# Latent attention weighed with the keys on the partitions, and retention's splits in another order: a two-block transformer forward on one core

## The chip, the cores and the metric

The kernel is one program on one core of a Trainium2 chip. The metric is the device time of one execution in microseconds (us), and the time of a kernel is the median of its runs. The engines are named as in the profile: PE (TensorE, matmuls), PEld (its weight loads), DVE (VectorE), ACT (ScalarE), POOL (GpSimd) and SP (SyncE, which issues most DMAs).

## The reference, cut to what matters

A first block of two layers is followed by a second block of two layers (short convolution, sparse attention, experts). The change touches the two mixers of the first block, on T = 16 + 512 = 528 tokens in float32:

```python
# layer 0: latent attention, 8 heads, 64 + 32 query/key dims, 64 value dims
q = (_rmsnorm(p_q, q_norm_g) @ w_uq); kv = (_rmsnorm(p_kv, kv_norm_g) @ w_ukv)
q = concat([q_nope, _rope(q_pe)]);  k = concat([k_nope, _rope(k_pe), one for all heads])
s = einsum('bqhd,bkhd->bhqk', q, k) * 96 ** -0.5;  s = where(kpos <= qpos, s, -1e30)
o = einsum('bhqk,bkhd->bqhd', softmax(s), v)
mix = concat([y_rec, o]) @ ev_w_out
# layer 1: retention, 4 heads of 256 query/key and 512 value dims
q, k = _rope(q), _rope(k) / 16
o = (q k^T * decay) v                      # kernel: over all 528 tokens at once
o = o * rsqrt(mean(o * o) + EPS);  mix = (silu(g) * o) @ od_w_out
```

## The kernel before, in words

Each engine has its own program, written as one function for each stage and engine (`mla_pe`, `mla_act`, `mla_dve`, `mla_pool` for latent attention, `ret_*` for retention, `out0_*` for the projection behind attention). An engine works in the order of its function, and semaphores join the engines. A `Signal.mark` says what an instruction has done and `wait_ge` waits for it. PSUM places are given out by a `Ring`: `take` waits until the last holder of the place is read out (`emptied`). `PS` are four places of two banks, `BANK` the eight single banks.

**Large products** (`dense`) run on weights split into a high and a low half. ACT casts a 128-column part of the loaded weights to its high half (`split_hi`), DVE subtracts it to get the low half (`split_lo`), and PE waits for the low half of each part. There are three places for parts (`WS`), and the splits run two parts ahead of PE: a call of `split_hi` and `split_lo` in an ACT or DVE function makes the next part in the list. Activations are split in the same way; `x_hi` and `x_lo` say when a row group is ready. The first two output tiles of a `dense` are done as a pair, row group k by row group k.

**Latent attention.** Features lie on the partitions. For each head PE projects q (96 rows) and k (64 rows), ACT copies them out, and PE turns q for the rotary part; DVE and POOL multiply, and DVE adds. All 8 heads are projected first, then v for five token blocks `TT` (four of 128 and one of 16). Then 40 query blocks x (head x // 5, block x % 5) go through a pipeline: scores for x + 3 (queries on the partitions), the mask, the row maximum and its scaling on DVE, the exponential with its sum on ACT into `P0` for x + 2, transposes of the probabilities on PE and the copy to `PT` on ACT for x + 1, and probabilities times v for x, one 64-column product per key block. DVE takes the reciprocal of the sum and scales the output into `OT`; every second head `turn_out_*` transposes 128 output features into place for `out0`.

**Retention**, for each head h: two q tiles, two k tiles, two plus two v tiles (`vg_cols`, first half), four g tiles, each 128 features wide; then transposes of v, scores, decay and the weighted sum. While head h starts, the output of head h - 1 is squared, normalised and multiplied into `YR` (POOL, `ret_scaled_pool`). Each engine then waits for these products (`pool_rot["y", h - 1, f]`), because `vT` is written again. DVE rotates q and k, and only then comes the loop over the v and g tiles with its splits. Behind head 3 the mean square goes through PE (`ret_norm_pe`), 16 row groups of `YR` are split into `HS` (k < 8) and `YS`, and the projection `("out", 1)` starts.

## Time and profile before

| | |
|---|---|
| median of 3 runs | 3312.5 us (3302.4 to 3315.7) |
| profiled execution, its own time | 3316.9 us |
| its span, first to last instruction | 3315.1 us |
| mean granted PE clock, of full speed | 0.936 |
| latent attention, first projection to the projection behind it | 132.98 to 294.77 us |
| of which projections of q, k and v | 132.98 to about 170 us |
| retention with its output projection's start | 749.61 to 1161.14 us |

Times in rows are microseconds from the span's start. Busy PE is not PE at its peak, because the ends of matmuls are modelled; the distance between starts says more. A float32 product counts as two matmul instructions. The granted clock is a share of 2.4 GHz, so 0.50 is 1.2 GHz. The number in square brackets or behind the second bar is the time an engine sat idle before the instruction, with what ended it.

### The profile page before, as it was taken

Reading aid. Unit: us, or ns where it says so; the run is one execution under the profiler, and the core shown is the slowest. Engines: PE = TensorE matmul, PEld = TensorE weight load, DVE = VectorE, ACT = ScalarE, POOL = GpSimd, SP = SyncE. Lnnn points to the kernel's source line nnn. Section 1 sums busy time; section 2 is a strip of 40 time slices with the busy share of each in tenths; the row PEclk is TensorE's granted clock in tenths of the full one; section 3 lists DMA queues with packets and bytes.
Section 4 is the critical chain, followed back from the end, with each engine's and each line's share of the span. In section 5 each row is a group of like instructions: output and inputs, shape, how many; then the busy total and the mean of one; then the engine's idle time right before and its main releaser. Section 6 shows DMA issues by size and latency. Waiting matters only on the chain.

```text
span 3315.1 us, 42753 instructions
## 1 busy us (share of the span) xinstructions
PE 2974.9 (90%) x17700; PEld 2318.1 (70%) x17700; DVE 1432.2 (43%) x2550; ACT 906.6 (27%) x1620; POOL 598.2 (18%) x529
## 2 busy tenths in 40 slices
PE   7899999999999899999999798888698897988884
PEld 6667999998887687888787455555476684555552
DVE  4543432334444434333444453333488845533334
ACT  3432422323222324232323121111334621211111
POOL 1201300112111012011200342222000002522220
PEclk9967899999999999999999899999899998999997
DMA  4010222222221132322222999999621019999996
GB/s 134 17 61 26 77 90 90 90 90 86 68 65 57 51 96 82 101 90 97 81 89 70 375 408 409 410 408 408 242 89 58 21 38 357 406 408 410 409 409 270
DMA packets 271813, 600.30 MB, mean 181 GB/s; under 512 B 32375, under 2 KB 177202, under 8 KB 255226
## 3 DMA queue, kind: packets, MB, share of 16 engines
q1 hardware_dynamic: 247408, 569.47, 45.6%
q0 software_dynamic: 23968, 27.93, 2.6%
q8 instruction: 144, 2.36, 0.3%
q14 instruction: 59, 0.48, 0.0%
q10 hardware_dynamic: 234, 0.06, 0.0%
HBM read 607.75 MB, written 39.89 MB: 195 GB/s over the span
## 4 chain that ended last, share of the span: by engine, by line
PE 85%; DVE 6%; issue 4%; DMA 2%; ACT 1%; POOL 1%; SPq 0%; DVEq 0%; POOLq 0%; ACTq 0%
PE ps L101 78%; PE ps L104 6%; POOL sb_arena L118 1%; DVE sb_arena L126 1%; DVE sb_tmpA L118 1%; DMA sb_ring<-in_exp_w_dram 1%; DVE sb_tmpA L126 1%; DVE sb_tmpA L122 1%; DVE sb_arena L118 0%; SPq L144 0%; DMA sb_arena<-x_rows,sb_smallu 0%; DVE sb_tmpA L2000 0%; ACT sb_hs L112 0%; DMA sb_arena<-in_ln_b_dram 0%; DVE sb_ws L118 0%
## 5 line engine op out<-in xcount | busy, mean ns | idle before, releaser
L101 PE MATMUL ps<-sb_hs,sb_ws 128*128 128x264 f32 (+1 forms) x6384 | 1117.3, 337 | 31.1 <-DVE sb_ws L118 17.6
L101 PEld LDWEIGHTS ps<-sb_hs,sb_ws 128*128 128x128 f32 x6384 | 982.7, 192 | 162.5 <-DVE sb_ws L118 18.5
L118 DVE TENSOR_TENSOR sb_ws<-sb_ring,sb_ws 128x1024 fp32r<-128x1024 f32 x279 | 367.6, 1321 | 433.9 <-ACT sb_ws L112 433.5
L101 PE MATMUL ps<-sb_arena 128*64 128x256 f32 (+16 forms) x2068 | 394.1, 438 | 48.5 <-issue 29.7
L112 ACT CAST sb_ws<-sb_ring 128x1024 fp32r<-128x1024 f32 x279 | 290.6, 1046 | 373.4 <-PE ps L101 355.4
L101 PE MATMUL ps<-sb_ring,sb_arena 128*64 128x256 f32 (+2 forms) x2314 | 324.0, 436 | 56.4 <-issue 55.2
L101 PE MATMUL ps<-sb_br,sb_ws 128*128 128x264 f32 (+1 forms) x2304 | 366.5, 321 | 0.0
L101 PEld LDWEIGHTS ps<-sb_br,sb_ws 128*128 128x128 f32 x2304 | 332.3, 188 | 33.7
L101 PEld LDWEIGHTS ps<-sb_arena 128*64 128x64 f32 (+6 forms) x2068 | 232.9, 170 | 154.0 <-issue 87.0
L101 PEld LDWEIGHTS ps<-sb_ring,sb_arena 128*64 128x64 f32 (+1 forms) x2314 | 196.7, 148 | 150.7 <-issue 88.8
L104 PEld LDWEIGHTS ps<-sb_cst,sb_arena 128*128 128x128 f32 (+3 forms) x1032 | 156.6, 206 | 195.7 <-DVE sb_arena L118 82.3
L101 PE MATMUL ps<-sb_hx,sb_arena 128*64 128x256 f32 (+1 forms) x1536 | 245.1, 470 | 27.4 <-issue 27.3
L108 ACT ACTIVATE sb_arena<-ps 64x256 f32<-64x256 f32 (+2 forms) x148 | 60.2, 407 | 765.0 <-PE ps L101 761.1
L118 DVE TENSOR_TENSOR sb_arena<-sb_arena,ps 64x256 f32<-64x256 f32 x128 | 54.3, 424 | 488.2 <-ACT sb_arena L108 488.2
L104 PE MATMUL ps<-sb_cst,sb_arena 128*128 128x128 f32 (+3 forms) x1032 | 203.2, 325 | 63.5 <-DVE sb_arena L123 22.1
L2448 POOL DMA_INDIRECT y_rows<-sb_arena,sb_smallu x128 | 134.6, 1052 | 660.9 <-PE ps L104 477.3
L112 ACT COPY sb_arena<-ps 128x128 f32<-128x128 f32 (+6 forms) x377 | 150.2, 435 | 328.3 <-PE ps L101 276.7
L101 PEld LDWEIGHTS ps<-sb_hx,sb_arena 128*64 128x64 f32 x1536 | 127.0, 144 | 102.8 <-issue 65.9
L118 POOL TENSOR_TENSOR sb_tmpA<-sb_tmpA 128x528 f32<-128x528 f32 (+1 forms) x88 | 103.2, 1173 | 461.6 <-ACT sb_tmpA L108 461.6
L115 DVE COPY sb_arena<-ps 64x512 f32<-64x512 f32 (+4 forms) x160 | 110.8, 695 | 152.9 <-PE ps L101 131.2
L2444 POOL DMA_INDIRECT sb_arena<-x_rows,sb_smallu x128 | 133.5, 1043 | 78.1 <-issue 35.6
L101 PE MATMUL ps<-sb_ys,sb_ws 128*128 128x512 f32 x576 | 139.3, 399 | 7.0 <-DVE sb_ws L118 7.0
(186 smaller groups left out, 2177.0 us busy)
## 6 DMA issues: line engine op xcount, KB each, us to landing
sb_ring<-in_exp_w_dram SPq DMA_DIRECT2D x160, 1024.0 KB
sb_hx<-in_exp_w_dram SPq DMA_DIRECT2D x128, 1024.0 KB
sb_arena<-in_exp_w_dram SPq DMA_DIRECT2D x96, 1024.0 KB
sb_ring<-in_mlp_w_dram SPq DMA_DIRECT2D x64, 1024.0 KB
sb_ring<-in_od_w_in_dram SPq DMA_DIRECT2D x24, 1024.0 KB
sb_ring<-in_conv_w_in_dram SPq DMA_DIRECT2D x12, 1024.0 KB
sb_ring<-in_attn_w_in_dram SPq DMA_DIRECT2D x10, 1024.0 KB
sb_ring<-in_od_w_out_dram SPq DMA_DIRECT2D x8, 1024.0 KB
```

The source lines that it names most:

```text
L101: return self.e.matmul(o, l, r, start=start, stop=stop, skip_group_check=True)
L104: return self.e.transpose(o, i, ident)
L108: return self.e.activation(o, i, fn, bias=bias, scale=scale)
L112: return self.e.copy(o, i)
L115: return self.e.tensor_copy(o, i)
L118: return self.e.tensor_tensor(o, a, b, op)
L122: return self.e.tensor_scalar(o, a, s1, None, op0)
L126: return self.e.scalar_tensor_tensor(out=o, in0=a, scalar=s, in1=b, op0=op0, op1=op1)
L2444: return e.e.indirect_dma_start(dst, None, Xh, bass.IndirectOffsetOnAxis(ap=ig[:, b:b + 1], axis=0), bounds_check=1023, oob_is_err=False)
L2448: return e.e.indirect_dma_start(Yh, bass.IndirectOffsetOnAxis(ap=isc[:, b:b + 1], axis=0), src, None, bounds_check=2047, oob_is_err=False)
```

## The change

Latent attention keeps the pass over query blocks, now 16 queries first and then four of 128 (`TQ`), but only for the maximum and the sum: the exponentials are thrown away. The logarithm of the sum is taken for four heads at a time (`ln`), joined with the maximum (`lse`), transposed to rows (`l`) and sent by DMA to partition 96 of q (`QH`); partition 96 of k (`KT`) holds ones. A second pass (`t`) computes the scores again with the keys on the partitions and 97 rows contracted, so that their exponential is the finished probability; three groups of key blocks a head. Step `o` multiplies v by them, with up to 264 queries moving, and `e` reads out two heads at once. Transposes of probabilities and outputs, their copies, the reciprocals and the scaling are gone. All engines follow one order, `mla_order`, in which the first pass of heads 0 to 3 lies between the projections.

In retention, the split of the third part behind the k tiles moves ahead of the wait for `pool_rot["y", ...]`. Behind head 3, row groups 0 to 7 are split before the outputs are copied, 8 to 11 before the normalisation, 12 to 15 after it, and `ret_norm_pe` runs inside the first pair of `("out", 1)`, at its row group 4. `ret_dve` gets the same edits as `ret_act`, with `split_lo` and `late_lo`. Below, the code is indented by 8 columns less, and the removed lines of latent attention are left out.

```diff
 def dense(e, stage, cols, K, rhs, T, units, pair=True, between=None):
...
         for k in range(kn + 2):
+            if k == 4 and between is not None:
+                between()
...
+PT = ar.take(2, 1360)
+triT = ar.take(128)
+LROW = tmpA[0:4, 2:4, :]
+rots = (tmpA[0:96, 5, :], tmpA[0:96, 4, :])
...
+TQ = [(0, 16)] + [(16 + 128 * i, 128) for i in range(4)]
+den, mxs, nms, lse = (sm[:, 100 + 40 * i:140 + 40 * i].rearrange("p (i h) -> p i h", i=5) for i in range(4))
+P_AT = (0, 528, 928, 1200, 1344)
...
+    t0, tn = TQ[i]
...
+def col(tile, x):
+    h, i, t0, tn, n = qblock(x)
+    return tile[0:tn, i, h:h + 1]
+def mla_order():
+    yield from (("q", 0), ("q", 1), ("turn", 0), ("q", 2), ("turn", 1))
+    for h in range(4):
+        for i in range(3):
+            yield "s", 5 * h + i
+        yield "q", h + 3
+        yield "s", 5 * h + 3
+        yield "turn", h + 2
+        yield "s", 5 * h + 4
+    yield from (("ln", 0), ("q", 7), ("turn", 6), ("v", 0), ("lse", 0), ("v", 1), ("turn", 7), ("l", 0))
+    yield from (("v", 2), ("v", 3), ("v", 4))
+    for x in range(20, 25):
+        yield "s", x
+    x = 25
+    for k in range(26):
+        if k < 24:
+            yield "t", k
+        if k == 7:
+            yield "lse", 1
+        for _ in range(3 - k % 2 if k < 6 else 0):
+            yield "s", x
+            x += 1
+        if k == 5:
+            yield "ln", 1
+        if k >= 2:
+            yield "o", k - 2
+        if k == 8:
+            yield "l", 1
+        if k >= 2 and k % 6 == 1:
+            yield "e", k // 6 - 1
...
+    proj = Ring([PS[0], PS[1]], U_, emptied)
+    rows = Ring([PS[2], PS[3]], U_, emptied)
+    cols = Ring([BANK[0], BANK[1]], U_, emptied)
+    outs = Ring([PS[1]], U_, emptied)
+    u = proj.take(e, "triT")
+    e.tp(u[:, 0:128], tri, ident).then_inc(*turned.mark("triT"))
...
+    for step, x in mla_order():
+        if step == "q":
+            u = proj.take(e, ("qh", x))
...
+            u = proj.take(e, ("kh", x))
...
+        if step == "turn":
+            u = proj.take(e, ("qturn", x))
+            e.wait_ge(*act_emptied["qh", x])
...
+                t = e.mm(o, rmat[0:96, 0:96], QH[0:96, x, a:b], True, True)
+            t.then_inc(*turned.mark(("qturn", x)))
+        if step == "v":
+            t0, tn = TT[x]
+            u = proj.take(e, ("vt", x))
...
+            if x == 4:
+                proj.drain(e)
+        if step == "s":
+            h, i, t0, tn, n = qblock(x)
+            u = rows.take(e, ("s", x))
...
+            t.then_inc(*scored.mark(("mla", x)))
+        if step == "l":
+            u = rows.take(e, ("lse", x))
+            e.wait_ge(*dve_soft["lse", x])
+            for i, (t0, tn) in enumerate(TQ):
+                at = t0 if i < 4 else 512
+                t = e.tp(u[0:4, at:at + tn], lse[0:tn, i, 4 * x:4 * x + 4], ident[0:tn, 0:tn])
+            t.then_inc(*turned.mark(("lse", x)))
+        if step == "t":
+            h, c = x // 3, x % 3
+            if x == 12:
+                rows.drain(e)
+                held = cols.holder
+                cols = Ring([BANK[0], BANK[1], BANK[6], BANK[7]], U_, emptied)
+                cols.holder[0:2] = held
+                outs = Ring([PS[2], PS[1]], U_, emptied)
+                outs.holder[1] = ("o", 1)
+            u = cols.take(e, ("t", x))
+            e.wait_ge(*pool_rot["one"])
+            e.wait_ge(*lse_in[h // 4][h])
+            K, Q1 = KT[0:97, h, :], QH[0:97, h, :]
+            if c == 0:
+                t = e.mm(u[:, 0:512], K[:, 0:128], Q1[:, 0:512], True, True)
+            if c == 1:
+                e.mm(u[:, 0:400], K[:, 128:256], Q1[:, 128:T1], True, True)
+                e.mm(u[:, 400:416], K[:, 0:128], Q1[:, 512:T1], True, True)
+                t = e.mm(u[0:16, 416:432], K[:, 512:T1], Q1[:, 512:T1], True, True)
+            if c == 2:
+                e.mm(u[:, 0:272], K[:, 256:384], Q1[:, 256:T1], True, True)
+                t = e.mm(u[:, 272:416], K[:, 384:512], Q1[:, 384:T1], True, True)
+            t.then_inc(*scored.mark(("t", x)))
+        if step == "o":
+            h, c = x // 3, x % 3
+            if h % 2 == 0 and c == 0:
+                u_o = outs.take(e, ("o", h // 2))
+            p0 = 64 * (h % 2)
+            (oa, _, _), (ob, _, _) = split(u_o, T1, p0, p0 + 64)
+            p = PT[:, h % 2, :]
+            e.wait_ge(*act_emptied["t", x if c else x + 1])
...
+                    e.wait_ge(*act_emptied["vt", j])
+            for j in ((0,), (1, 4), (2, 3))[c]:
+                q0, jn = 128 * j, TT[j][1]
+                v, pj = Vt[0:jn, j, 64 * h:64 * h + 64], p[0:jn, P_AT[j]:P_AT[j] + T1 - q0]
+                if q0 < 264:
+                    e.mm(oa[:, q0:264], v, pj[:, 0:264 - q0], j == 0, j == 2)
+                a = max(q0, 264)
+                t = e.mm(ob[:, a - 264:264], v, pj[:, a - q0:T1 - q0], j == 0, j == 3)
...
+    cols.drain(e)
+    units.n = 2
+    units.holder[1] = ("o", 3)
...
+    for step, x in mla_order():
+        if step == "q":
+            if x == 0:
+                e.wait_ge(*turned["triT"])
+                e.acp(triT, U_["triT"][:, 0:128]).then_inc(*act_emptied.mark("triT"))
+            e.wait_ge(*summed["qh", x])
+            e.acp(halves(QH[0:96, x, :]), whole(U_["qh", x], T1, 0, 96)).then_inc(*act_emptied.mark(("qh", x)))
+            e.wait_ge(*summed["kh", x])
+            e.acp(halves(KT[0:64, x, :]), whole(U_["kh", x], T1, 0, 64)).then_inc(*act_emptied.mark(("kh", x)))
+        if step == "v":
+            tn = TT[x][1]
+            e.wait_ge(*summed["vt", x])
+            e.acp(Vt[0:tn, x, :], U_["vt", x][0:tn, 0:512]).then_inc(*act_emptied.mark(("vt", x)))
+        if step == "s":
+            h, i, t0, tn, n = qblock(x)
+            e.wait_ge(*dve_soft["max", x])
+            if x >= 2:
+                e.wait_ge(*act_emptied["s", x - 2])
+            e.act(tmpA[0:tn, x % 2, 0:n], U_["s", x][0:tn, 0:n], ACT.Exp, scale=SC96, bias=col(nms, x),
+                  acc=col(den, x)).then_inc(*act_emptied.mark(("s", x)))
+        if step == "ln":
+            e.wait_ge(*act_emptied["s", 20 * x + 19])
+            d = den[:, :, 4 * x:4 * x + 4]
+            e.act(d, d, ACT.Ln).then_inc(*act_soft.mark(("ln", x)))
+        if step == "l":
+            u = U_["lse", x]
+            e.wait_ge(*turned["lse", x])
+            e.acp(LROW[:, x, 0:400], u[0:4, 0:400]).then_inc(*act_emptied.mark())
+            e.acp(LROW[:, x, 400:T1], u[0:4, 512:640]).then_inc(*act_emptied.mark(("lse", x)))
+            e.wait_ge(*act_emptied["lse", x])
+            for i in range(4):
+                h = 4 * x + i
+                e.dma(QH[96:97, h, :], LROW[i:i + 1, x, :]).then_inc(
+                    *lse_in[x].land(*(range(4 * x, 4 * x + 4) if i == 3 else [])))
+        if step == "t":
+            h, c = x // 3, x % 3
+            u, p = U_["t", x], PT[:, h % 2, :]
+            e.wait_ge(*dve_soft["mask", x])
+            if h >= 2:
+                e.wait_ge(*weighed["mla", 3 * h - 4])
+            if c == 0:
+                e.act(p[:, 0:512], u[:, 0:512], ACT.Exp, scale=SC96).then_inc(*act_emptied.mark(("t", x)))
+            if c == 1:
+                e.act(p[:, 528:928], u[:, 0:400], ACT.Exp, scale=SC96).then_inc(*act_emptied.mark())
+                e.act(p[:, 512:528], u[:, 400:416], ACT.Exp, scale=SC96).then_inc(*act_emptied.mark())
+                e.act(p[0:16, 1344:1360], u[0:16, 416:432], ACT.Exp, scale=SC96).then_inc(
+                    *act_emptied.mark(("t", x)))
+            if c == 2:
+                e.act(p[:, 928:1344], u[:, 0:416], ACT.Exp, scale=SC96).then_inc(*act_emptied.mark(("t", x)))
+        if step == "e":
+            e.wait_ge(*weighed["mla", 6 * x + 5])
+            e.acp(halves(HS[:, 0, 4 + x, :]), whole(U_["o", x], T1)).then_inc(*x_hi.mark(("mix0", 4 + x)))
...
+    e.mset(sm[:, 100:260], 1.0).then_inc(*dve_soft.mark())
+    e.wait_ge(*dve_soft.now)
+    for step, x in mla_order():
+        if step == "q":
+            if x == 0:
+                e.wait_ge(*dve_lru["kpe"])
+            e.cp(KT[64:96, x, :], kpe[64:96, :]).then_inc(*dve_soft.mark(("kpe", x)))
+        if step == "turn":
+            rot = rots[x % 2]
+            e.wait_ge(*turned["qturn", x])
+            if x > 1:
+                e.wait_ge(*dve_soft["q", x - 2])
+            e.tt(halves(rot), whole(U_["qturn", x], T1, 0, 96), halves(S96[0:96, :]), ALU.mult).then_inc(
+                *dve_emptied.mark(("qturn", x)))
+            e.wait_ge(*dve_emptied["qturn", x])
+            e.wait_ge(*pool_rot["q", x])
+            e.tt(QH[0:96, x, :], QH[0:96, x, :], rot, ALU.add).then_inc(*dve_soft.mark(("q", x)))
+        if step == "s":
+            h, i, t0, tn, n = qblock(x)
+            u = U_["s", x]
+            e.wait_ge(*scored["mla", x])
...
+            e.rmax(col(mxs, x), u[0:tn, 0:n]).then_inc(*dve_soft.mark())
...
+            e.ts(col(nms, x), col(mxs, x), -SC96, None, ALU.mult).then_inc(*dve_soft.mark(("max", x)))
+        if step == "lse":
+            g = slice(4 * x, 4 * x + 4)
+            e.wait_ge(*act_soft["ln", x])
+            e.stt(lse[:, :, g], den[:, :, g], -1.0 / SC96, mxs[:, :, g], ALU.mult, ALU.subtract).then_inc(
+                *dve_soft.mark(("lse", x)))
+        if step == "t":
+            u = U_["t", x]
+            e.wait_ge(*scored["t", x])
+            e.wait_ge(*act_emptied["triT"])
+            e.tt(u[:, 0:128], u[:, 0:128], triT, ALU.add).then_inc(
+                *dve_soft.mark(*([("mask", x)] if x % 3 == 0 else [])))
+            if x % 3 == 1:
+                e.tt(u[0:16, 416:432], u[0:16, 416:432], triT[0:16, 0:16], ALU.add).then_inc(
+                    *dve_soft.mark(("mask", x)))
+            if x % 3 == 2:
+                e.tt(u[:, 272:400], u[:, 272:400], triT, ALU.add).then_inc(*dve_soft.mark(("mask", x)))
+        if step == "e":
+            hi, lo = HS[:, 0, 4 + x, :], HS[:, 1, 4 + x, :]
+            e.wait_ge(*x_hi["mix0", 4 + x])
+            e.tt(halves(lo), whole(U_["o", x], T1), halves(hi).bitcast(F), ALU.subtract).then_inc(
+                *dve_emptied.mark(("o", x)))
...
+    e.wait_ge(*dve_lru["h", 3])
+    e.mset(KT[96:97, :, :], 1.0).then_inc(*pool_rot.mark("one"))
+    for step, x in mla_order():
+        if step == "turn":
+            e.wait_ge(*turned["qturn", x])
+            e.tt(QH[0:96, x, :], QH[0:96, x, :], C96[0:96, :], ALU.mult).then_inc(*pool_rot.mark(("q", x)))
...
+        x_lo["mix0", k] if k < 4 else dve_emptied["o", k - 4])
...
-    ret_norm_pe(e, units, 3)
-    dense_all(e, ("out", 1), C4, 16, mix1_x, T2, units)
+    dense_all(e, ("out", 1), C4, 16, mix1_x, T2, units, True, lambda: ret_norm_pe(e, units, 3))
...
 def ret_act(e):
+    def late_hi(ks):
+        for k in ks:
+            e.wait_ge(*pool_rot["y", k // 4, k % 4])
+            e.acp(late(mix1_of(k, 0)), late(YR[:, k, :])).then_inc(*x_hi.mark(("mix1", k)))
+
...
+        split_hi(e)
         if h > 0:
             for f in range(4):
                 e.wait_ge(*pool_rot["y", h - 1, f])
-        for m in tiles(vg_cols(h)):
-            split_hi(e)
+        for n, m in enumerate(tiles(vg_cols(h))):
+            if n > 0:
+                split_hi(e)
...
+        if h == 3:
+            late_hi(range(8))
         for f in range(4):
             e.wait_ge(*weighed["ret", h, f])
...
     ret_squares_act(e, 3)
-    for k in range(8):
-        e.wait_ge(*weighed["ret", 3, 3])
-        e.wait_ge(*pool_rot["y", k // 4, k % 4])
-        e.acp(late(HS[:, 0, k, :]), late(YR[:, k, :])).then_inc(*x_hi.mark(("mix1", k)))
+    late_hi(range(8, 12))
     ret_scaled_act(e, 3)
...
+    late_hi(range(12, 16))
     for m in range(8):
         out_splits(e, split_hi, m)
         square_act(e, ("out", 1), m, 2)
```

## Rows read from the trace of the kernel before

**Rows 1.** The page: the span, and the engines' shares of the chain that ended last.

```profile
span 3315.1 us, 42753 instructions
...
PE 85%; DVE 6%; issue 4%; DMA 2%; ACT 1%; POOL 1%; SPq 0%; DVEq 0%; POOLq 0%; ACTq 0%
```

**Rows 2.** TensorE in order of time, stretches of latent attention: start, length, [idle before].

```profile
138.38 2.98 PE L101 MATMUL ps<-sb_arena,sb_ring 128*96 128x264 f32 x12
141.29 1.13 PE L101 MATMUL ps<-sb_arena,sb_cst 96*96 96x264 f32 x4
...
173.90 1.12 PE L101 MATMUL ps<-sb_arena 96*128 96x512 f32 x2
174.86 0.38 PE L104 MATMUL ps<-sb_cst,sb_arena 128*128 128x128 f32 x2
...
294.77 35.47 PE L101 MATMUL ps<-sb_hs,sb_ws 128*128 128x264 f32 x276 [1.43 <-DVE sb_hs L118]
```

**Rows 3.** Windows: length, busy us (instructions) by engine, PE clock, DMA share, GB/s.

```profile
133.00:170.00 37.00, 35.62 (x138) 20.23 (x138) 20.04 (x32) 12.72 (x21) 11.76 (x9) 1.00 0.09 29
170.00:184.00 14.00, 11.64 (x71) 7.55 (x70) 9.11 (x36) 6.18 (x21) 0.00 (x0) 1.00 0.95 301
206.00:240.00 34.00, 31.99 (x121) 21.69 (x121) 13.35 (x54) 10.47 (x33) 0.00 (x0) 0.50 0.00 1
294.80:298.00 3.20, 3.20 (x14) 3.20 (x15) 1.23 (x1) 0.12 (x1) 0.00 (x0) 0.50 0.00 0
298.00:301.00 3.00, 3.00 (x26) 3.00 (x26) 0.00 (x0) 0.00 (x0) 0.00 (x0) 0.99 0.00 0
882.40:892.00 9.60, 9.60 (x56) 9.60 (x57) 3.51 (x4) 0.68 (x1) 0.00 (x0) 0.68 0.34 111
2540.00:2580.00 40.00, 33.08 (x211) 24.45 (x211) 34.23 (x133) 25.67 (x72) 2.68 (x5) 1.00 0.16 41
```

**Rows 4.** Groups of VectorE instructions from 133 to 295 us, by shape.

```profile
L118 DVE TENSOR_TENSOR ps<-ps,sb_cst 128x128 f32<-128x128 f32 x32 | 9.3, 289 | 16.1 <-PE ps L101 16.1
L138 DVE TENSOR_REDUCE sb_small<-ps 16x1 f32<-16x528 f32 x8 | 5.6, 695 | 0.3
L122 DVE TENSOR_SCALAR sb_small<-sb_small 128x1 f32<-128x1 f32 x32 | 4.9, 153 | 1.1
L118 DVE TENSOR_TENSOR sb_arena<-ps,sb_arena 96x528 f32<-96x528 f32 x4 | 2.8, 704 | 5.0 <-PE ps L101 5.0
```

**Rows 5.** Groups of ScalarE instructions from 133 to 295 us, by shape.

```profile
L109 ACT ACTIVATION_READ_ACCUMULATOR sb_arena<-ps,sb_small 128x1 f32 x32 | 6.2, 194 | 0.0
L109 ACT ACTIVATE sb_arena<-ps,sb_small 128x512 f32<-128x512 f32 x8 | 5.5, 687 | 2.2 <-DVE sb_small L122 2.2
```

**Rows 6.** Groups of GpSimd instructions from 133 to 295 us, by shape.

```profile
L118 POOL TENSOR_TENSOR sb_arena<-sb_arena 96x528 f32<-96x528 f32 x8 | 10.4, 1306 | 22.3 <-PE ps L101 22.3
```

**Rows 7.** Retention in order of time, VectorE and TensorE: start, length, [idle before].

```profile
881.13 1.21 DVE L118 TENSOR_TENSOR sb_ws<-sb_ring,sb_ws 128x1024 fp32r<-128x1024 f32 x1
...
882.40 36.99 PE L101 MATMUL ps<-sb_hs,sb_ws 128*128 128x264 f32 x192 [5.88 <-DVE sb_ws L118]
...
1077.78 36.58 PE L101 MATMUL ps<-sb_hs,sb_ws 128*128 128x264 f32 x192 [5.88 <-DVE sb_ws L118]
```

**Rows 8.** The end of retention in order of time, all engines.

```profile
1139.58 2.04 PE L101 MATMUL ps<-sb_tmpA,sb_cst 128*128 128x512 f32 x2 [5.43 <-DVE sb_tmpA L118]
...
1142.88 1.28 ACT L108 ACT_TABLE_LOAD   x1
1144.17 0.69 ACT L108 ACTIVATE sb_tmpA<-ps,sb_small 128x512 f32<-128x512 f32 x1
1144.89 3.35 DVE L129 RECIPROCAL sb_tmpA<-sb_tmpA 128x512 f32<-128x512 f32 x1 [0.64 <-ACT sb_tmpA L108]
1149.05 6.74 POOL L118 TENSOR_TENSOR sb_arena<-sb_arena,sb_tmpA 128x512 f32<-128x512 f32 x4 [73.64 <-DVE sb_tmpA L118]
...
1161.14 9.24 PE L101 MATMUL ps<-sb_ys,sb_ws 128*128 128x512 f32 x31 [7.03 <-DVE sb_ws L118]
```

190 lines of the change are left out of this document (27 added, 163 removed).

## The prediction

> **What bounds the kernel.** I read the page first: the chain that ended last is 85% PE, and DVE's 6% comes next [rows 1]. So a stage gains from less PE time, or from a wait of PE that goes; DVE or ACT work counts only where PE waits for it. Next I read PE in order of time. Latent attention takes 132.98 to 294.77 us, 161.8 us. Then the windows: the projections run at clock 1.00, the pipeline of query blocks begins at 1.00, and from about 185 us it is at 0.50, 1.2 GHz, nearly to its end [rows 3]. Its PE is 94% busy there with 64-column products and transposes. The reader should see that the same work at full clock would take about half as long. Two other stretches help to judge: the second block's attention, PE 83% busy with short waits, stays at 1.00; and behind latent attention the clock is back 3 to 4 us after a dense stream starts [rows 3]. In retention PE waits 5.88 us for a split of weights before its third v or g part, for heads 1, 2 and 3, and restarts at a low clock [rows 7, 3]; at the end it waits 5.43 and 7.03 us [rows 8].
>
> **Attention, the price list.** A float32 product of 512 columns is two instructions, 0.48 us each from start to start [rows 2]; that is 1.88 ns a column and product with overhead. New PE work for a head: first pass 16 + 144 + 272 + 400 + 528 = 1360 columns, 2.7 us; second pass 512 + 432 + 416 = 1360 columns, 2.6 us; v times probabilities 1360 columns, 2.7 us. The last two have products of 8 and 16 columns whose weight loads bound them, so I take 2.8 each. Before, the first pass had 1808 columns. The projections cost 2.98 + 0.98 us a head as before [rows 2]. DVE for a first-pass block: mask 0.29, maximum 0.70 for 528 columns, scaling 0.15, with gaps 1.25 [rows 4]; 1.15, 1.0, 0.85 and 0.55 for the shorter ones. ACT: exponential 0.69 + 0.19 for the sum [rows 5].
>
> **Attention, walked through.** *Start, 13 us.* The first eviction waits behind other ACT work to 136.8 us as now; two places for projections instead of four cost about 1 us more. The ones' memset lies in GpSimd's idle time before the first turn; without that cover I bound it by one pass of its 96x528 multiply for each head's row, 10 us, and by nothing, and take nothing. *Heads 0 to 3, 10 us each.* There are two places for scores. In a head: PE does block 2, block 3, the projections (2.98), block 4 and the turn by 5.7 us. DVE has finished block 4 at 5.9 and works on the turn: 0.70, then it waits for GpSimd, whose 1.31 ends at 7.05 [rows 6], and 0.70 more, 7.8. Queued behind is block 5: DVE to 9.05, ACT to 10.0. Only then is the place free for the next head's block 2. PE works 6.8 us of the 10. Its idle 3 us sit at the end. *Between, 13 us of PE time from 182.8.* ACT needs the logarithm's table, 1.28 us [rows 8]; head 7's projections and turn and v follow, with their copies on ACT in one queue with four row DMAs; v's last copy ends at 196. *Head 4's first pass, then heads 5 to 7 mixed with t and o, 34 us.* Each block goes PE, DVE, ACT, two places, and t's mask and exponential stand in the same queues; two heads' worth of blocks (13 us and 9 us by the walk) bound it, and two table loads, 2.6 us, lie in it. *The rest, 34 us.* 18 steps of t and o at 1.87 us, PE bound, because masks (0.3 to 0.6) and exponentials (0.7 to 1.1) fit into the two steps between. The output's readout (ACT 0.6, DVE 0.7) is now hidden by the next projection's first four row groups; before, PE waited for it. Without that cover it is 1.4 us [rows 2].
>
> Sum: 13 + 40 + 13 + 34 + 34, less 3 us of overlap of the second and third, is 131, against 161.8: 31 us less if the clock stays at 1.00. It will not quite. Each 3 us wait of a head's end is like those before which the clock fell; at half clock until a dense stream has run 4 us, it costs 2 us. Four heads 8 us at most, the mixed part as much. I take 10 of 0 to 16. The projection behind starts at full instead of half clock (3.2 us at 0.50 and part of a fourth) and gains 2. **Attention: 23 us, between 10 and 33.** The row DMAs: the price of a small SBUF to SBUF transfer isn't in the trace. Between nothing and 8 us each, the first is hidden by v and head 4's blocks (9 us), the second by four steps (7 us); at the upper bound it costs 1 us.
>
> **Table loads against a page.** The load before the square root takes 1.28 us, and the next activation starts 1.29 us after it began [rows 8]. The Trainium skill, "ScalarE: Activation LUTs", section "What ACT_TABLE_LOAD costs", adds a drain and gives about 2.66 us a switch; four switches between Exp and Ln would cost 10.6 us of ACT by it and 5.2 us by the row. The same page's section on table sets says one set holds both functions, which would leave one switch.
>
> **Retention.** The split that PE waits for is made by DVE at 881.13, behind the rotation of q and k, and PE starts 1.2 us later [rows 7]. Moved ahead of the wait for GpSimd's products, its conditions (loaded weights, and a place that is free since the second k tile, two tiles earlier) are long met, and DVE only waits there for GpSimd, so its 1.2 us delay nothing. If POOL's traffic doubles it, 1.1 us goes to the rotation. PE then goes on at 876.5 (882.40 less 5.88) with the third part, 6.1 us to 882.5. The fourth part is late next: DVE ends the rotation at 881.2, copies v (0.7), splits (1.2): 883.2. New wait 0.8 instead of 5.88: 5.1 us, three times, 15.2. And the clock: 882.4 to 892 has 0.68, a loss of 3.1 us [rows 3]; head 3's stretch is 0.4 us shorter, 2.7 us [rows 7]. At 2.5 each, 7.5 us. Head 0 has no such wait. *Behind head 3:* the first 8 row groups are split in idle time of ACT and DVE. So PE starts the projection at 1134.2 (1139.58 less 5.43), does four row groups (20 products of 0.22, 4.3 us), waits 1 us for the squares (DVE ends them at 1139.5 either way) and goes on to 1146.6. The second half needs parts split behind the last row groups. ACT begins the root at 1141 instead of 1142.9, since four casts stand before it; the reciprocal ends 1146.4, GpSimd's fourth product 7.5 us after (as before, from the end of the reciprocal), 1153.9, DVE's last low half 1155.2, the weights' split 1156.4. That is 4.7 us before 1161.14 [rows 8]. PE's wait grows to 10 us there though the gain is real: a wait is no loss in itself. **Retention: 15.2 + 7.5 + 4.7 = 27 us, between 5 and 32.**
>
> **The sum.** 3316.9 - 23 - 27 = 3267 for the profiled execution's own time, which is 4.4 us above the median; so **3262.5 us** on the median. The stages between and behind are PE dense or start their transfers relative to these stages, so the shift reaches the end.
>
> **Rivals.** (a) *The clock stays at 1.2 GHz through the new attention.* For it: it did so for 100 us with PE busy 94% [rows 3]. Against: the second block's attention, less busy, held 1.00; the new products stream 264 to 512 columns. Price: a head of the first part becomes 15.4 us, the mixed part 52, the last 67; attention about 204 us, 42 more than before, and with retention's 27 the time is 3328. It decides from an attention of 189 us on. This is the other sign: 0.07. (b) *DVE and ACT take all that PE gives back*: the first pass's blocks and turns queue more than I walked, attention stays at 162, only retention gains, 3285: 0.13. (c) *Retention's wait only moves to the fourth part*, 5 us again, attention gains: 3285: 0.08. It needs a rotation 4 us later than now, for which I see nothing. (d) *The clock stays at 1.00 throughout and nothing is lost*: 31 + 2 + 27 = 60, 3252: 0.10. The clock with transposes at 170 to 184 us and in the second block was 1.00 [rows 3], so transposes alone don't explain the low clock, and I give (d) no more. The Trainium skill, "TensorE: Matmul & The Clock Gate", Part 4 (PE-mode transpose), says that transposes don't count as activity for the clock; if that were the whole cause, removing them would give (d). (e) *My forecast*, 3245 to 3277: 0.62.
>
> **Range and chances.** Faster than 3296 (0.5%, about what a measurement of this kernel can tell): (b) to (e) with a little of each falling short, 0.92. Within 0.5%: 0.04, from (b) and (c) together. Slower: half of (a), 0.04. The range that keeps 8 in 10 leaves out (a), the upper half of (b) and (c), and the tip of (d): 3243 to 3288.
>
> **What would show it.** In the profile after: attention 132.98 to about 272 us; PE idle about 3 us at each of four heads' ends, ended by ACT's exponential; in the last part PE without gaps at clock 0.95 or more, steps of 1.9 us. In retention no idle over 2 us before heads 1 to 3's third and fourth parts, with clock 1.00; one PE wait of about 10 us, ended by a split, before `sb_ys` products. I am wrong if the last part of attention shows 0.50, if t waits for the row DMAs, or if a PE wait of 5 us stands before the fourth part.

## The result, and the profile after

The changed kernel takes **3287.0 us** (median of 7 runs, 3282.5 to 3288.9), the kernel before 3312.5 us (7 runs on the same chip, 3300.0 to 3315.7). The ratio is 0.9932, with a 95% interval from 0.9916 to 0.9949: 25 us or 0.7% faster, where 50 us were forecast. The profiled execution takes 3288.9 us, 1.9 us above the median, and its span is 3287.1 us. The direction held and so did the range, 3243 to 3288, by 1 us; the size was half of what I forecast. Attention gave nearly nothing instead of 23 us, and retention gave 25 us instead of 27.

The page first: the span, and the shares of the chain that ended last. PE has 82% of it where it had 85%, and DVE 7% where it had 6% [rows 1].

```profile
span 3287.1 us, 42420 instructions
...
PE 82%; DVE 7%; issue 4%; DMA 3%; ACT 2%; SPq 1%; POOL 1%; ACTq 0%; DVEq 0%; POOLq 0%
```

TensorE of the changed kernel in order of time, the starts of attention's stretches and what it waited for:

```profile
133.62 0.33 PE L104 MATMUL ps<-sb_cst 128*128 128x128 f32 x1 [0.70 <-ACT sb_arena L108]
...
149.84 1.27 PE L101 MATMUL ps<-sb_arena 96*128 96x272 f32 x2 [2.50 <-ACT sb_tmpA L109]
...
162.07 1.56 PE L101 MATMUL ps<-sb_arena 96*128 96x144 f32 x4 [2.97 <-ACT sb_tmpA L109]
...
173.51 1.75 PE L101 MATMUL ps<-sb_arena 96*128 96x144 f32 x4 [2.98 <-ACT sb_tmpA L109]
...
186.09 1.68 PE L101 MATMUL ps<-sb_arena 96*128 96x144 f32 x4 [2.98 <-ACT sb_tmpA L109]
...
261.96 32.40 PE L101 MATMUL ps<-sb_arena 97*128 97x512 f32 x152
```

Windows of the same kernel (length, busy us by engine, granted clock, DMA share, GB/s):

```profile
162.00:173.50 11.50, 8.43 (x28) 5.15 (x28) 5.87 (x18) 4.02 (x14) 1.30 (x1) 0.81 0.00 0
...
194.20:211.60 17.40, 12.14 (x36) 5.49 (x36) 5.11 (x10) 6.87 (x15) 3.10 (x3) 0.86 0.18 61
211.60:221.60 10.00, 8.82 (x18) 3.93 (x18) 5.07 (x20) 4.93 (x14) 0.00 (x0) 0.50 1.04 330
221.60:240.00 18.40, 17.95 (x38) 9.66 (x39) 8.20 (x30) 6.27 (x21) 0.00 (x0) 0.50 0.16 50
240.00:260.40 20.40, 19.34 (x63) 10.75 (x61) 7.55 (x28) 9.14 (x24) 0.00 (x0) 0.65 0.00 0
261.40:294.30 32.90, 32.90 (x159) 18.72 (x158) 7.05 (x27) 10.24 (x29) 0.00 (x0) 1.00 0.00 1
294.30:301.00 6.70, 6.70 (x56) 6.70 (x56) 1.93 (x2) 1.55 (x2) 0.00 (x0) 1.00 0.00 0
```

What to see: the end of attention, t and o alone, is as forecast, 32.9 us without a gap at full clock, and the projection behind it starts at full clock instead of 0.50 [rows 3]. But attention takes 160.7 us (133.62 to 294.28) against 161.8. In heads 0 to 3 PE waits 2.5 to 3.0 us in each for ACT, and the clock is 0.8. In the mixed part, where the first pass of heads 4 to 7 runs between steps t and o, PE hardly waits at all: 17.95 of 18.40 us are busy, but at 1.2 GHz. That is what the old pipeline looked like at 206 to 240 us [rows 3].

Retention in the changed kernel, TensorE:

```profile
877.87 28.42 PE L101 MATMUL ps<-sb_hs,sb_ws 128*128 128x264 f32 x144 [1.44 <-DVE sb_ws L118]
...
1060.18 28.41 PE L101 MATMUL ps<-sb_hs,sb_ws 128*128 128x264 f32 x144 [1.44 <-DVE sb_ws L118]
...
1108.31 4.91 PE L101 MATMUL ps<-sb_hs,sb_ws 128*128 128x512 f32 x20
1114.10 1.10 PE L101 MATMUL ps<-sb_tmpA,sb_cst 128*128 128x512 f32 x2 [0.88 <-DVE sb_tmpA L118]
1114.63 7.04 PE L101 MATMUL ps<-sb_hs,sb_ws 128*128 128x512 f32 x28
1131.08 13.23 PE L101 MATMUL ps<-sb_ys,sb_ws 128*128 128x512 f32 x48 [9.41 <-DVE sb_ws L118]
```

Each wait of 5.88 us [rows 7] has become one of 1.44 us, before the fourth part, and a head is 6 to 7 us shorter. The lead over the kernel before is 5.3 us where retention starts (744.35 against 749.61), 30.1 us at the projection's second half (1131.08 against 1161.14 [rows 8]) and 28.0 us at the end of the span. Of the 5.3 us, the profiled attention gave 0.5. Another 1.5 had come by the end of the projection behind it (341.34 against 343.29), which is the clock at the projection's start, where I forecast 2. Another 3.0 came in the normalisation that follows (352.45 against 357.36). That code is unchanged; from 347 to 357 us it ran at a clock of 0.68 in this execution and of 0.50 in the one before, so these 3 us are not a gain of attention's own work.

### The profile page after: what moved, and what is told of

Its sections match the earlier page's. It is cut to its first block, busy times and chain, and to the rows that moved or that the text cites. A ratio compares the mean times of both kernels' runs of the same rounds, so it can differ in the third digit from the quotient of the medians.

```text
span 3287.1 us, 42420 instructions
## 1 busy us (share of the span) xinstructions
PE 2953.0 (90%) x17555; PEld 2285.1 (70%) x17555; DVE 1430.0 (44%) x2508; ACT 912.2 (28%) x1628; POOL 601.0 (18%) x530
## 4 chain that ended last, share of the span: by engine, by line
PE 82%; DVE 7%; issue 4%; DMA 3%; ACT 2%; SPq 1%; POOL 1%; ACTq 0%; DVEq 0%; POOLq 0%
PE ps L101 77%; PE ps L104 5%; DMA sb_ring<-in_exp_w_dram 1%; DVE sb_tmpA L118 1%; SPq L144 1%; DVE sb_arena L126 1%; DMA sb_hx<-in_exp_w_dram 1%; DVE sb_tmpA L126 1%; DVE sb_ws L118 1%; DVE sb_arena L118 1%; DVE sb_tmpA L129 1%; POOL sb_arena L118 1%; DMA sb_arena<-x_rows,sb_smallu 0%; DVE sb_tmpA L2095 0%; DVE sb_tmpA L122 0%
## 5 line engine op out<-in xcount | busy, mean ns | idle before, releaser
L101 PEld LDWEIGHTS ps<-sb_hs,sb_ws 128*128 128x128 f32 x6384 | 972.1, 190 | 147.6 <-issue 14.0
L108 ACT ACTIVATE sb_arena<-ps 64x256 f32<-64x256 f32 (+6 forms) x188 | 73.7, 403 | 792.4 <-PE ps L101 762.8
L104 PEld LDWEIGHTS ps<-sb_cst,sb_arena 128*128 128x128 f32 (+2 forms) x912 | 137.1, 206 | 183.5 <-DVE sb_arena L118 82.2
L104 PE MATMUL ps<-sb_cst,sb_arena 128*128 128x128 f32 (+2 forms) x912 | 176.0, 321 | 64.1 <-DVE sb_arena L123 22.7
L112 ACT COPY sb_arena<-ps 128x128 f32<-128x128 f32 (+5 forms) x335 | 137.4, 449 | 293.2 <-PE ps L101 278.5
L115 DVE COPY sb_arena<-ps 64x512 f32<-64x512 f32 (+3 forms) x155 | 107.7, 695 | 154.5 <-PE ps L101 133.1
```

Source lines behind the costliest of these rows:

```text
L101: return self.e.matmul(o, l, r, start=start, stop=stop, skip_group_check=True)
L104: return self.e.transpose(o, i, ident)
L108: return self.e.activation(o, i, fn, bias=bias, scale=scale)
L112: return self.e.copy(o, i)
L115: return self.e.tensor_copy(o, i)
```

## The experiments

Each kernel is the changed kernel with the edit shown, unless something else is said. Ratios are to the kernel before on the same chip, with their 95% interval.

**1. The two parts apart.** The first of these has the new attention and the old retention, the second the old attention and the new retention.

```diff
 # first kernel: the changed kernel without these and their like in ret_dve
-    dense_all(e, ("out", 1), C4, 16, mix1_x, T2, units, True, lambda: ret_norm_pe(e, units, 3))
+    ret_norm_pe(e, units, 3)
+    dense_all(e, ("out", 1), C4, 16, mix1_x, T2, units)
...
-        split_hi(e)
         if h > 0:
             for f in range(4):
                 e.wait_ge(*pool_rot["y", h - 1, f])
-        for n, m in enumerate(tiles(vg_cols(h))):
-            if n > 0:
-                split_hi(e)
+        for m in tiles(vg_cols(h)):
+            split_hi(e)
```

> The new latent attention with retention as before. If the change's parts simply add, this gains what the profile after shows up to retention's start, about 5 us, with the first layer's attention still about 160 us long: near 3307 us. The forecast's 23 us would give 3290. Rival: the parts hinder each other (later weight loads, for one), and alone the attention gains 10 us or more.

> Retention's new order with latent attention as before. By the profile after, retention gives 25 us: near 3288 us, three waits of about 1.4 us in place of 5.9, and clock 1.00 behind them. If part of it belonged to the attention (weights loaded earlier), less than 20 us.

New attention alone: 3315.2 us, ratio 1.0006 (0.9987 to 1.0025). New retention alone: 3288.9 us, 0.9939 (0.9916 to 0.9963). So retention gives the whole gain that can be seen; attention gives at most 4 us by its interval, and not the 5 us that I had expected from the profile. Windows of the kernel with new attention only, in the mixed part:

```profile
211.60:221.60 10.00, 7.70 (x15) 3.42 (x16) 3.84 (x14) 5.01 (x12) 0.00 (x0) 0.62 0.75 248
221.60:240.00 18.40, 17.75 (x42) 9.16 (x40) 9.00 (x34) 7.22 (x24) 0.00 (x0) 0.56 0.29 95
240.00:260.40 20.40, 18.39 (x80) 10.42 (x80) 8.36 (x32) 10.92 (x29) 0.00 (x0) 0.92 0.00 1
```

The same code got its clock back sooner here, and its attention took 156.7 us (134.07 to 290.76) instead of 160.7. The old attention varies too: 161.8 us in the profile of before and 157.3 us (132.24 to 289.58) in the second kernel. These pairs differ by 4 to 5 us, and a third profile of the new attention (experiment 6) lies 8 us below the first, so one profile can't price this stage; it takes the medians to judge it.

**2. Give PE wide products to do where it waits.** The rival to test was that ACT and DVE bound attention, so that the clock only follows. Unread products of 512 columns, on a weight part and a row group that lie ready, go into a place before the program waits for it: 12 before the next head's block 2, 8 twice in the part between, 4 before each block of head 4 and 2 before each of head 5. They are 82 in all, 36 before the heads and 46 later; the texts below, on record, count 76 and 40.

```diff
+    def burn(place, held, n):
+        p = e.part
...
+        for _ in range(n):
+            e.mm(place[:, 0:512], halves_of(p)[0][:, 0, :], HS[:, 0, 0, 0:512], True, True)
+    def spare(ring, n):
+        i = ring.n % len(ring.places)
+        burn(ring.places[i], ring.holder[i], n)
     for step, x in mla_order():
+        if step == "s" and x < 20 and x % 5 == 1 and x > 1:
+            spare(proj, 12)
+        if step == "turn" and x == 6:
+            spare(rows, 8)
+        if step == "v" and x == 4:
+            spare(rows, 8)
+        if step == "s" and 20 <= x < 30:
+            burn(PS[1], None, 4 if x < 25 else 2)
```

> The changed kernel with extra products of 512 columns whose results nobody reads, put where TensorE waits in the first pass: 12 before the second block of heads 1 to 3, 8 before head 6's turn, 8 before v's last block, 4 before each block of head 4 and 2 before each of head 5. They add 76 products of 0.22 us, 17 us of TensorE work. Clock theory (the missing time is TensorE at 1.2 GHz): the clock stays near 1.00 from 162 to 260 us, the stretch from the first block to the last part shrinks by 10 to 20 us in spite of the extra work, 3267 to 3277 us. Queue theory (VectorE and ScalarE in order, with two places for scores, bound that stretch): the time stays or grows by up to 10 us, 3287 to 3297, though the clock rises.

3274.2 us, ratio 0.9890 (0.9854 to 0.9927): 13 us less than the changed kernel, though PE has some 20 us more to do (82 products of 0.25 us). The two ratios' intervals touch, but each of the four runs (3268.6 to 3277.1) lies below each run of the changed kernel. TensorE in order of time, and windows:

```profile
163.56 1.40 PE L101 MATMUL ps<-sb_arena 96*128 96x512 f32 x6
164.89 3.02 PE L101 MATMUL ps<-sb_hs,sb_ws 128*128 128x512 f32 x12
167.93 0.97 PE L101 MATMUL ps<-sb_arena 96*128 96x144 f32 x4
...
177.70 0.97 PE L101 MATMUL ps<-sb_arena 96*128 96x144 f32 x4
...
199.84 1.17 PE L101 MATMUL ps<-sb_hs,sb_ws 128*128 128x512 f32 x4 [0.76 <-ACT sb_arena L112]
...
213.63 2.09 PE L101 MATMUL ps<-sb_arena 96*128 96x512 f32 x10
```

```profile
162.00:174.00 12.00, 11.94 (x48) 7.72 (x49) 7.10 (x22) 4.71 (x14) 1.74 (x2) 1.00 0.00 0
199.80:213.60 13.80, 13.76 (x58) 9.44 (x59) 7.26 (x28) 6.36 (x21) 0.00 (x0) 1.00 0.95 305
222.00:240.00 18.00, 16.48 (x68) 9.39 (x66) 8.24 (x31) 10.37 (x27) 0.00 (x0) 0.90 0.00 0
```

The 12 products fill exactly the 3 us that PE waited. A head now takes 9.8 us (167.93 to 177.70) where it took 11.4 to 12.6, and attention 141.9 us (132.44 to 274.38). ACT and DVE have the same work as in the changed kernel, so their work alone doesn't set its time; with the waits filled the clock is 1.00 and the stage is shorter. In the mixed part the filler stands from 199.84 to 213.6 us, at clock 1.00. The window from 222 to 240 us lies behind it and holds no filler: it runs at 0.90.

**3. Which half of the filler matters.** Only the 36 products before the heads, and only the 46 later ones.

```diff
 # heads only: of the four conditions above, this one stays
+        if step == "s" and x < 20 and x % 5 == 1 and x > 1: spare(proj, 12)
 # late only: the other three stay
```

> As the filler run, with only the 12 products before the second block of heads 1 to 3; none between the parts and none in the mixed part. The clock stays at 1.00 to about 185 us and a head takes 9.8 us, as in the filler run. Clock theory: the waits of 2.4 and 2.2 us behind it (for copies on ScalarE) still throw the clock to 0.50, and the mixed part takes 49 us as in the changed kernel: 6 us of the filler's 20 in the profile, near 3281 us. If instead the clock, once kept, survives the short waits, the whole 20 are there, 3267 to 3274.

> The kernel after, with the unread 512-column products only between the two parts and in the mixed part (40 of the 76), none before the heads. If each stretch's clock follows only what ran just before and in it, then heads 0 to 3 stay at 11.4 to 12.6 us and a clock of 0.8, the mixed part (212 to 240 us) rises from 0.50 to 0.85 or more, and the time is 9 us below the kernel after (the filler everywhere gave 13, that of the heads alone 4), 3278. If the mixed part can only keep a clock that the heads hand over, it stays at 0.50 to 0.6, and the added products make the time 3285 to 3292.

Heads only: 3282.7 us, 0.9912 (0.9883 to 0.9942). Late only: 3283.0 us, 0.9903 (0.9886 to 0.9921). Windows, heads only and then late only:

```profile
162.00:174.00 12.00, 11.94 (x52) 7.79 (x51) 6.95 (x24) 4.91 (x18) 1.30 (x1) 1.00 0.00 0
...
194.00:212.00 18.00, 14.06 (x32) 6.29 (x32) 5.63 (x16) 6.35 (x15) 2.60 (x2) 0.69 0.29 95
222.00:240.00 18.00, 16.73 (x53) 9.09 (x52) 9.24 (x35) 7.32 (x25) 0.00 (x0) 0.69 0.00 0
```

```profile
162.00:173.50 11.50, 8.48 (x27) 4.87 (x27) 4.98 (x16) 3.48 (x10) 1.31 (x1) 0.80 0.00 0
211.60:221.60 10.00, 10.00 (x43) 6.59 (x41) 6.07 (x23) 4.73 (x18) 0.00 (x0) 1.00 1.03 326
221.60:240.00 18.40, 16.21 (x64) 9.17 (x63) 10.75 (x40) 7.73 (x28) 0.00 (x0) 0.91 0.00 1
```

In these two runs the clock of a stretch follows what PE does in it and just before. Heads with the filler run at 1.00 and hand over a full clock, and the waits of the part between lose it again; with the filler there (208.35 to 222 us) the mixed part runs at 1.00, and at 0.91 behind it, though the heads stay at 0.8. DMA moves as much there (326 GB/s) as in the changed kernel at 0.50 (330 GB/s), so its traffic isn't what lowers the clock. The gains are 4 and 4 us, and the intervals of both ratios overlap that of the changed kernel; for the late half I expected 9. By the profiles, attention is 150.0 and 149.1 us, 3 to 12 us less than in three profiles of the changed kernel's code (below). With the filler in one half only, the waits of the other half lose the clock again, which is seen for the heads-only kernel at 194 us.

Stage by stage, from the starts of matmuls, the unfilled code varies more in the mixed part than anywhere else:

| us | heads 0 to 3 | between | mixed part |
|---|---|---|---|
| changed kernel | 47.5 | 17.5 | 49.8 |
| new attention only (experiment 1) | 48.1 | 17.2 | 43.9 |
| split early (experiment 6) | 45.9 | 17.3 | 43.7 |
| filler everywhere | 38.6 | 15.8 | 41.7 |
| filler at the heads only | 41.4 | 18.8 | 43.9 |
| filler late only | 46.0 | 15.7 | 40.9 |

My 9 for the late half was only the 13 of the whole filler less the 4 of the heads. Against the second and third row, which are the changed kernel's attention too, the late filler gives 3 us in the mixed part and 1.5 in the part between, which fits the 4 on the median. The 13 us of the whole filler, from four runs, is good to about 6 us by the spread of the runs, so 13 and the sum of 8 don't contradict each other. Nor does any run show the mixed part at full clock without added products: some 8 of its 41 us are then the 30 added products' own time.

**4. As busy, but narrow.** If it were enough that PE is busy, any product would do. Each filler of 512 columns becomes two of 16 columns on the same weights; at full clock such a pair takes as long as the wide one (24 narrow products 2.85 us, against 3.02 for 12 wide), at half clock it takes nearly twice as long (8 narrow products 1.77 us from 213.87).

```diff
-            e.mm(place[:, 0:512], halves_of(p)[0][:, 0, :], HS[:, 0, 0, 0:512], True, True)
+            for _ in range(2):
+                e.mm(place[:, 0:16], halves_of(p)[0][:, 0, :], HS[:, 0, 0, 0:16], True, True)
```

> As the filler run, in the same places, but each product of 512 columns replaced by two of 16 columns on the same 128-column weights, which should take TensorE about as long at full clock (0.11 us each, bound by the weight loads). TensorE is as busy and as seldom idle, but streams few columns. If idle time alone lowers the clock, it stays at 1.00 and the time is 3267 to 3277 as with the wide filler. If streamed columns count, the clock falls as in the changed kernel, and with the filler's own time doubled at 1.2 GHz the run is no faster than it: 3285 to 3295.

3299.3 us, 0.9972 (0.9956 to 0.9988): 12 us slower than the changed kernel, a little more than I had expected, and 25 slower than with the wide filler. TensorE, then windows:

```profile
160.94 2.85 PE L101 MATMUL ps<-sb_hs,sb_ws 128*128 128x16 f32 x24
163.99 1.75 PE L101 MATMUL ps<-sb_arena 96*128 96x144 f32 x4 [0.21 <-ACT sb_tmpA L109]
...
213.87 1.85 PE L101 MATMUL ps<-sb_hs,sb_ws 128*128 128x16 f32 x8 [0.76 <-ACT sb_arena L112]
...
238.51 4.03 PE L101 MATMUL ps<-sb_arena 96*128 96x512 f32 x10
```

```profile
174.00:186.00 12.00, 11.97 (x48) 8.30 (x48) 5.23 (x17) 3.96 (x12) 1.31 (x1) 0.72 0.01 1
213.90:238.50 24.60, 24.60 (x88) 19.89 (x89) 7.53 (x29) 6.64 (x21) 0.00 (x0) 0.50 0.53 172
```

PE waits only 0.21 us at the head's end, and the clock from 162 to 194 us is still 0.72 to 0.86. Where the filler stands in the mixed part, PE is busy for all of 24.60 us by the profile, at half clock. The same ten blocks with their fillers, from the first filler to the products behind the last, take 24.6 us here (213.87 to 238.51) and 13.8 us with the wide filler (199.84 to 213.63). Removing the wait alone does not keep the clock; what stands in its place matters. A narrow pair has fewer columns than a wide product and also twice the weight loads; which of the two counts was not separated. The old pipeline, 94% busy with 64-column products at 0.50 [rows 3], fits this, but no run tests it there.

**5. Shorten the wait instead of filling it.** Two edits. A third place for scores, so that PE needn't wait for the exponential of block 5:

```diff
-    rows = Ring([PS[2], PS[3]], U_, emptied)
+    rows = Places([BANK[4], BANK[5], PS[3]], U_, emptied)
...
-            u = rows.take(e, ("s", x))
+            u = rows.take_at(e, (0, 1, 0, 1, 2)[x % 5], ("s", x))
```

> The changed kernel, with three places for first-pass scores instead of two: two single banks for blocks 1 to 4 of a head and the two-bank place for block 5, so that block 2 of the next head no longer waits for block 5's exponential. Both theories expect TensorE's 3 us waits at the heads' ends to shrink. Queue theory: a head of the first part falls from 11.9 to about 9.5 us, 8 us less in all, and the mixed part gains 5: 3274 us. Clock theory: the same 8 us and, with the waits gone, a clock near 1.00 in that part, which keeps the mixed part from starting slow only if the waits between are short too; these remain, so the mixed part stays at 0.50 and gains nothing: 3279 us.

And the last block ahead of the turn, because the turn's two DVE passes and its wait for GpSimd hold up the block's mask:

```diff
-        yield "turn", h + 2
         yield "s", 5 * h + 4
+        yield "turn", h + 2
```

> The changed kernel with the turn of head h + 2 behind block 5 of head h instead of ahead of it, so that VectorE does block 5 first. By the walk, block 5's exponential ends 2 us earlier, the next head's second block starts 2 us earlier, but its third waits for its first, whose mask then stands behind the turn: a head falls from 11.9 to about 11 us, TensorE's wait from 3.0 to about 2, and the clock is still lost. 3 to 4 us less than the changed kernel, near 3283. If the order of VectorE's queue were the main cause of the missing 22 us, 10 us less or more.

Third place: 3290.6 us, 0.9937 (0.9912 to 0.9963), no gain, where I had expected 8 us or more by either theory. The wait has only moved one block on:

```profile
162.74 1.21 PE L101 MATMUL ps<-sb_arena 96*128 96x272 f32 x2 [2.89 <-ACT sb_tmpA L109]
```

Block 3 goes into the place of block 1 of the same head, whose mask stands in DVE's queue behind the last head's block and turn. A place more doesn't help while the reader's queue is the same. Turn last: 3283.9 us, 0.9916 (0.9886 to 0.9946), 3 us less on the median, with an interval that overlaps the changed kernel's, so the gain isn't clear of noise. One wait of 3.0 us has become two of 1.03 and 1.37.

**6. Retention's end.** PE's 9.41 us wait before the second half ends with a split of weights. VectorE of the changed kernel there:

```profile
1125.27 4.62 DVE L118 TENSOR_TENSOR sb_ys<-sb_arena,sb_ys 128x512 fp32r<-128x512 f32 x4
1129.81 3.48 DVE L118 TENSOR_TENSOR sb_ws<-sb_ring,sb_ws 128x1024 fp32r<-128x1024 f32 x3
```

The weight part that all of the second half needs, row groups 8 to 11 too, is split behind the last four row groups. One part is split early instead:

```diff
     if h == 3:
         late_hi(range(8))
+        split_hi(e)
...
-        out_splits(e, split_hi, m)
+        out_splits(e, split_hi, m, 1 if m == 0 else 0)
```

The last argument says how many splits fewer are made there; `ret_dve` gets the same edit with `split_lo`.

> The kernel after, with one edit in retention: the first weight part of the output projection is split right behind row groups 0 to 7 instead of behind the twelfth to fifteenth, so that the first pair of output tiles needs one part less behind the wait for GpSimd's products. If the wait before the projection's second half is set by the split that stands last in VectorE's queue, the wait of 9.4 us becomes one of 2 to 3 us (the rest is the products themselves) and the time falls by 3 to 7 us against the kernel after, to about 3281 on its median. If GpSimd's products alone set it, nothing changes, 3287.

3282.2 us, 0.9912 (0.9896 to 0.9927), 5 us less than the changed kernel on the median. The intervals overlap; what is clear is the place itself. TensorE:

```profile
1103.16 4.91 PE L101 MATMUL ps<-sb_hs,sb_ws 128*128 128x512 f32 x20
...
1116.08 3.40 PE L101 MATMUL ps<-sb_ys,sb_ws 128*128 128x512 f32 x14
1121.71 0.97 PE L101 MATMUL ps<-sb_ys,sb_ws 128*128 128x512 f32 x3 [2.23 <-DVE sb_ys L118]
1123.40 8.88 PE L101 MATMUL ps<-sb_ys,sb_ws 128*128 128x512 f32 x31 [0.72 <-DVE sb_ys L118]
1132.12 11.28 PE L101 MATMUL ps<-sb_hs,sb_ws 128*128 128x512 f32 x48
```

The first pair takes 29.0 us (1103.16 to 1132.12) instead of 35.8 (1108.31 to 1144.15). PE does four row groups while GpSimd and DVE finish the rest. This profile's attention, the changed kernel's own code, took 152.8 us (132.36 to 285.21): the third value for it beside 160.7 and 156.7.

**7. All that helped, together.** The filler (8 instead of 12 before a head), the turn last, `("q", 7)` before `("ln", 0)`, two of the five copies of v on DVE, and the early split.

```diff
-    yield from (("ln", 0), ("q", 7), ("turn", 6), ("v", 0), ...
+    yield from (("q", 7), ("ln", 0), ("turn", 6), ("v", 0), ...
...
-        if step == "v":
+        if step == "v" and x % 2 == 0:      # mla_act; the others are copied in mla_dve
```

> A version that should beat both: the filler, 8 instead of 12 products at the heads' ends, with the turn behind block 5; head 7's projections copied before the logarithm; two of v's five copies on VectorE; and behind retention's head 3 the next part of the projection's weights split right behind row group 7, so that the second half starts on row groups 8 to 11 without waiting for the normalisation. Against the filler run: about 1 us a head, 3 to 4 us between the parts, 3 to 4 us at retention's end: 3262 to 3268 us. Its latent attention should end near 268 us and the wait before the YS products fall from 9.4 to about 6 us. Retention's part shows by itself in the profile; the rest would be lost if the clock falls with the smaller filler.

**3261.5 us**, 0.9848 (0.9822 to 0.9874): 50 us below the kernel before and 25 below the changed kernel. Its profiled execution took 3272.3 us, 11 more than its median. The first pair took 29.0 us in it again (1097.33 to 1126.34), with waits of 2.23 and 0.72 us where I had expected about 6. Its attention ended at 283.31 and not near 268, as I had expected. The filler's stretch ran at 1.00 as in experiment 2, but behind it, where both kernels do the same work, the clock fell:

```profile
222.00:240.00 18.00, 17.47 (x43) 9.42 (x42) 5.82 (x22) 5.08 (x17) 0.00 (x0) 0.50 0.00 1
```

Experiment 2 had 0.90 in the stretch behind its filler. So even the wide filler does not hold the clock of the mixed part in every execution. What each edit to the order gives beside filler and split was not measured.

## Why the prediction was wrong in size, by its own steps

**Attention: the step that failed is the clock term, "I take 10 of 0 to 16".** The walk without it was 131 us. Measured against it, in the profile after: the start is 13.2 us (13 forecast) and the rest 32.9 (34). Heads 0 to 3 take 47.4 us (146.8 to 194.2) and not 40, the part between 17.4 and not 13, the mixed part 49.8 (211.6 to 261.4) and not 34, and the 3 us of overlap did not come: 13.2 + 47.4 + 17.4 + 49.8 + 32.9 = 160.7. Nearly 30 us over the walk, where I allowed 10. In the other two profiles of the same code it is 26 and 22 us.

The reason I gave for the size of the term fails first. I tied the loss to the waits of 3 us, "like those before which the clock fell". In the kernel before, no such wait stood there. The longest between 171 us and the fall near 185 us is this one:

```profile
185.29 1.86 PE L101 MATMUL ps<-sb_arena 96*16 96x512 f32 x4 [1.37 <-ACT sb_arena L109]
```

So a stretch of small products with short waits was enough there, and the mixed part is such a stretch.

- Heads: the wait of 3 us at each end was forecast, and came. The loss of about 2 us a head came as well, 7.4 in all and so nearly the whole of the "8 us at most". With the wait filled a head takes 9.8 us at full clock, so the walk's 10 was right, and right that the clock is the difference.
- Mixed part: this is the larger miss, 16 us here and 10 in the other two profiles. I had put the clock's loss here at "as much" as in the heads and had then taken not quite two thirds of both. It stayed at 0.50 for 28 us and at 0.65 for 20 more. PE's waits there are only 0.16 to 0.76 us, with products of 16 to 512 columns between. The wide filler ran at 1.00, and the stretch behind it at 0.90 in one profile and 0.50 in another (experiment 7). How much of the 10 to 16 us is clock and how much a walk that was too short stays open, since no run shows the part at full clock without filler. Rival (a), the low clock, was thus half true of this part, and I had given it 0.07 because I tied it to the whole stage: it priced the mixed part at 52 us, and 49.8, 43.9 and 43.7 were measured. It was false of the last part.
- Between: a term was missing. The chain that ended last runs here through ACT, ScalarE of the changed kernel in order of time (ACTq is the issue of DMAs):

```profile
197.50 1.28 ACT L108 ACT_TABLE_LOAD   x1
198.79 0.22 ACT L108 ACTIVATE sb_small<-sb_small 128x20 f32<-128x20 f32 x1
...
206.31 2.54 ACTq L144 DMA_DIRECT2D sb_arena<-sb_tmpA  x4
208.89 1.07 ACT L112 COPY sb_arena<-ps 128x512 f32<-128x512 f32 x2 [2.61 <-issue]
...
211.53 1.28 ACT L109 ACT_TABLE_LOAD   x1
```

I had asked how long the row DMAs take to land, and t never waited for them. What they cost is 2.54 us of ACT's queue for four issues, with the copies of v, and so PE, behind them: PE waits 2.20 us at 209.53. The table load and the logarithm, with the copies behind them, cost another 2.36 us of PE's time at 199.55.

**Table loads against the page.** The load before the logarithm begins at 197.50 and the logarithm at 198.79, 1.29 us later. So this trace agrees with the row that I had used and shows nothing behind the load; the Trainium skill, "ScalarE: Activation LUTs", section "What ACT_TABLE_LOAD costs", adds a drain of 1.38 us that isn't seen here. Exp and Ln did not share a set: a load stands before each of the four changes between them (at 197.50, 211.53, 255.11 and 256.64), though the same page's section on table sets lists one set that holds both.

**Rival (d) and the transposes.** The new attention has no transposes of probabilities, and its clock was still 0.50 for 28 us. As I had held, the rule of the Trainium skill, "TensorE: Matmul & The Clock Gate", Part 4 (PE-mode transpose), that transposes don't count as activity, can't be the whole cause here.

**Rival (b)** named nearly the right number, 3285, by the wrong way, so its hit would have been luck: it had DVE and ACT take what PE gives back. Experiment 2 leaves their work as it is and makes attention 11 to 19 us shorter than in three profiles of the new code.

**Retention: right.** Forecast 15.2 + 7.5 for three heads; measured 19.9 from the head periods (98.3, 97.1 and 98.0 us before; 91.2, 91.1 and 91.2 after). The new wait is 1.44 us instead of 0.8, which is 1.9 of the 2.8 us missing. At the end 4.7 were forecast and 4.2 came (1134.18 to 1161.14 is 27.0 us, 1108.31 to 1131.08 is 22.8), with the wait forecast at 10 at 9.41 and the one for the squares at 0.88 instead of 1. I had named the weights' split behind the last low half as the end of the chain without asking whether it must stand there; experiment 6 shows that 6.9 us of the first pair lay in that place in the profile, and some 5 on the median.

**The sum.** 25.5 us on the medians is retention's 24 (the second kernel of experiment 1) and next to nothing else. That the new attention was 5.5 us ahead of before in its own profile up to 1807 us, 4.7 at 2365 and 0.7 at the end stays open; the clock of the second block differs a little between executions (0.95 and 0.93 from 2500 to 3260 us in those two), and one profile of each can't separate that.

## What to carry to other kernels

Before counting on less PE work in a stage, write its clock beside it, stretch by stretch: here a stage of short bursts stayed at 1.2 GHz for 28 us, and cutting its PE work bought nothing that the medians show, while wide products in its waits, though nobody reads them, bought 13 us. Useful wide work in that place should do better; no run here tried it. When a wait ends in a split or copy that depends on nothing late, look where it stands in its engine's queue: moving one such instruction forward gave 4.4 us a head in the change and 5 us in experiment 6, while a further buffer only moved the wait, because the same queue stood behind it. A DMA issued by a busy engine costs that engine its issue time, here 0.6 us each, even when nobody waits for it to land.

## What the runs showed of the hardware that I had not expected

- Filling PE's time isn't enough for its clock. With products of 16 columns in its waits PE was busy 24.60 of 24.60 us at 0.50 in the mixed part; with products of 512 columns in the same places it was busy 13.76 of 13.80 us at 1.00, for the same ten blocks. Adding 20 us of the wide ones made the kernel 13 us faster, the narrow ones 12 us slower.
- The same code in the same stage took 160.7, 156.7 and 152.8 us in three executions, with the clock from about 222 to 240 us at 0.50, 0.56 and 0.69. The largest part of the difference is the mixed part's 49.8, 43.9 and 43.7 us. A stage that changes between the two levels of the clock has no single time, and one profile of it can mislead: the changed kernel's own was the slowest of the three.
